# Recurrence matrices stored dense per state group, their products as 64 by 64 parts of the array, lag matrices spread by transfers

## What is computed

```python
def s5_mixer(u, lam_re, lam_im, log_dt, b_re, b_im, c_re, c_im, d, w_glu, b_glu):
    uf = u.astype(f32).reshape(bsz, L, S5_GROUPS, S5_GROUP)
    y = uf * d.astype(f32).reshape(S5_GROUPS, S5_GROUP)
    for direction in range(2):
        ...
        bu = jnp.einsum('blgh,gph->blgp', uf, b_bar)
        a = jnp.broadcast_to(lam_bar, bu.shape)
        _, state = lax.associative_scan(_linear_recurrence_op, (a, bu), axis=1,
                                        reverse=(direction == 1))
        ...
        y = y + jnp.real(jnp.einsum('blgp,ghp->blgh', state, c_mat))
    y = jax.nn.gelu(y.reshape(bsz, L, W_A))
```

## Time and profile before

| | |
|---|---|
| runs | 2553.88 us median, 2548.26 to 2555.88 (3 runs) |
| the profiled execution | 2550.92 us, its span 2549.4 us |
| mean granted TensorE clock | 0.991 |
| busy share: TensorE, its weight loads, VectorE, ScalarE, GpSimd | 98%, 81%, 72%, 50%, 6% |
| TensorE's share of the chain that ended last | 94% |
| HBM traffic | 161 GB/s over the span |

### The profile page before, as it was taken

One profiled execution on the slowest core, in us unless ns is written; L12 is line 12 of the kernel. 1 busy time (PEld: TensorE's weight loads), 2 busy tenths in 40 slices (PEclk: granted clock), 3 DMA queues, 4 the chain that ended last, 5 costly groups with the idle time before them and its releaser, 6 DMA issues.

```text
span 2549.4 us, 44643 instructions
## 1 busy us (share of the span) xinstructions
PE 2487.7 (98%) x15016; PEld 2053.9 (81%) x15016; DVE 1846.8 (72%) x3235; ACT 1273.7 (50%) x2364; POOL 142.6 (6%) x270
## 2 busy tenths in 40 slices
PE   6999999999999999999989999999999999999998
PEld 5888888887777778898778888888777777788986
DVE  7888888745777776556678888886367877765666
ACT  5556556634444444453465655555344434354535
POOL 2110000100000000000021000010000000000000
PEclk9999999999999999999999999999999999999998
DMA  7545445443454435555565544544444534365554
GB/s 253 175 157 165 160 160 164 152 147 136 156 168 134 138 110 187 189 173 175 166 206 162 164 160 159 167 156 145 149 151 150 175 112 149 115 193 189 171 177 145
DMA packets 117959, 411.86 MB, mean 162 GB/s; under 512 B 16484, under 2 KB 18586, under 8 KB 117584
## 3 DMA queue, kind: packets, MB, share of 16 engines
q1 hardware_dynamic: 107424, 391.17, 46.4%
q0 software_dynamic: 10416, 19.16, 2.3%
HBM read 403.97 MB, written 6.29 MB: 161 GB/s over the span
## 4 chain that ended last, share of the span: by engine, by line
PE 94%; DVE 3%; issue 2%; ACT 1%; PEldq 0%; DMA 0%; PEld 0%; DVEq 0%; ACTq 0%; POOL 0%; POOLq 0%
PE bank L1620 30%; PE bank L1660 21%; PE bank L1662 10%; PE bank L2008 7%; PE bank L1595 5%; PE bank L1577 4%; PE bank L1928 2%; PE bank L1793 2%; PE bank L1715 1%; PE bank L1698 1%; PE bank L1751 1%; PE bank L1942 1%; PE bank L1826 1%; PE bank L1908 1%; PE bank L1850 1%
## 5 line engine op out<-in xcount | busy, mean ns | idle before, releaser
L388 ACT ACTIVATE WH<-ring 128x512 fp32r<-128x512 f32 x1364 | 851.8, 631 | 1061.2 <-PE bank L1620 471.6
L402 DVE TENSOR_TENSOR WL<-ring,WH 128x512 fp32r<-128x512 f32 x852 | 573.3, 689 | 410.5 <-ACT WH L388 407.8
L1660 PE MATMUL bank<-XX,WH 128*128 128x512 f32 x2304 | 825.7, 402 | 29.4 <-DVE XX L573 15.2
L1662 PE MATMUL bank<-XX,WL 128*128 128x256 f32 x2304 | 646.3, 280 | 0.0
L1660 PEld LDWEIGHTS bank<-XX,WH 128*128 128x128 f32 x2304 | 436.0, 189 | 139.4 <-issue 18.8
L1620 PE MATMUL bank<-WH,XX 128*128 128x512 f32 x1536 | 487.4, 399 | 4.5 <-issue 3.4
L393 DVE TENSOR_TENSOR WL<-ring,WH 128x512 fp32r<-128x512 f32 x512 | 349.4, 688 | 122.5 <-ACT WH L388 117.2
L1662 PEld LDWEIGHTS bank<-XX,WL 128*128 128x128 f32 x2304 | 437.9, 190 | 0.0
L1620 PEld LDWEIGHTS bank<-WH,XX 128*128 128x128 f32 x1536 | 286.3, 189 | 82.3 <-issue 22.7
L1620 PE MATMUL bank<-WL,XX 128*128 128x512 f32 x768 | 300.6, 391 | 0.0
L1620 PEld LDWEIGHTS bank<-WL,XX 128*128 128x128 f32 x768 | 144.7, 188 | 31.4
(11 more groups left out here) (316 smaller groups left out, 3232.3 us busy)
## 6 DMA issues: line engine op xcount, KB each, us to landing
ring<-in_blocks SPq DMA_DIRECT2D x738, 512.0 KB, 3.3
ARENA<-in_bc POOLq DMA_DIRECT2D x2, 2048.0 KB, 8.3
ARENA<-in_decay POOLq DMA_DIRECT2D x8, 512.0 KB, 4.1
ARENA<-in_x SPq DMA_DIRECT2D x4, 512.0 KB, 8.2
u_scratch<-ARENA POOLq DMA_DIRECT2D x16, 128.0 KB, 3.0
ARENA<-u_scratch POOLq DMA_DIRECT2D x64, 32.0 KB, 2.9
y_scratch<-ARENA POOLq DMA_DIRECT2D x16, 128.0 KB, 2.7
ARENA<-y_scratch POOLq DMA_DIRECT2D x128, 16.0 KB, 2.0
```

The source lines that it names most:

```text
L388: nc.scalar.activation(wh[q], raw(which[0], q), ACT.Copy).then_inc(wh_ready[q], 1)
L402: vec.tensor_tensor(wl[q], raw(which[0], q), wh[q].bitcast(F32), ALU.subtract).then_inc(w_used[slot(which[0], half)], 1)
L1660: ins = mm(bank[b][:, :], h, xx[:, :, k, :], start=(k == 0), stop=(k == DT - 1), skip_group_check=True)
L1662: ins = mm(bank[b][:, 0:T], l, xh[:, k, :], start=False, stop=(k == DT - 1), skip_group_check=True)
```

## The change

It changes how the matrices of the recurrence stand in SBUF and in which parts of the array they are multiplied:

- E and F are stored dense: the two groups of a pair stand in the upper and lower 64 partitions, with the same columns. The zeros are gone; VectorE makes each part with one operation over 128 partitions where it took two over 64. Only the first step of E keeps a padded copy, EZ, for the lags (ScalarE, four small copies `first_step` per pass).
- The channels of a projection tile are permuted on the host (`by_class`) so that pairs 0, 2 stand in one half of the partitions and pairs 1, 3 in the other. `U4` is filled with 8 transfers per tile where there were 4, issued behind the write of the next tile.
- `turn()` makes 16 transposes of 64 rows, 64 wide, in one go; two evictions where there were four. `inputs()`, `direct()` and `outputs()` multiply 64 by 64 parts with 64 columns, dealt over the halves of rows and columns. Banks 2 and 3 now go by class and no more by real and imaginary part, so VectorE's rotation reads and writes with other strides.
- `lags()` is 64 wide. ScalarE evicts the 7 lags in one copy (LAG), GpSimd writes them to `lag_scratch` and reads them back with 8 transfers into M. The 16 window copies are gone.
- The direct part stands by itself between blocks 6 and 7, into banks 6 and 7. Waits of the interludes are put ahead of the last pair of the block before (`ahead`).

The order on TensorE becomes `block_at(0)`, `block_at(1)`, `turn()`, `block_at(2)`, `inputs()`, `block_at(3)`, `lags()`, `block_at(4)`, `block_at(5)`, `block_at(6)`, `direct()`, `block_at(7)`, `outputs()`.

```diff
-        E, ET, F, M = area(90, 8), area(98, 4), area(102, 10), area(112, 2)
+        E, EZ, ET, F, M = area(90, 4), area(94, 2), area(98, 4), area(102, 5), area(112, 1)
+        LAG = area(96, 1)[:, 0:LAGS * 16]
...
+                def load_input(m):
+
+                    pool.wait_ge(us_written[m % 2], layer * (8 * WT) + 16 * (m // 2 + 1))
+                    pool.sem_inc(us_landed, 1)
+                    by_step = u_scratch[layer, m].rearrange("(s n h) (t c) -> s t h n c", s=2, n=4, t=STEP)
+                    for s_ in range(2):
+                        for t in range(STEP):
+                            rows = slice(64 * s_ + 16 * t, 64 * s_ + 16 * t + 16)
+                            pool.dma_start(split(U4[rows, m * T:(m + 1) * T], 4), by_step[s_, t]).then_inc(u4_loaded, 16)
...
-                    pool.wait_ge(psum_free[7], read_out(layer, "s5", 7, ct))
+                    pool.wait_ge(psum_free[4], read_out(layer, "s5", 4, ct * 2 + 1))
+                    pool.dma_start(lag_scratch[ct], LAG).then_inc(lag_written, 16)
+                    pool.wait_ge(lag_written, layer * (16 * WT) + (ct * 16 + 16))
+                    by_half = lag_scratch[ct].rearrange("(s n h) x -> s h n x", s=2, n=4)
+                    for s_ in range(2):
+                        for t in range(STEP):
+                            rows = slice(64 * s_ + 16 * t, 64 * s_ + 16 * t + 16)
+                            pool.dma_start(split(M[rows, :], 4), by_half[s_][:, :, (STEP - 1 - t) * 16:(2 * STEP - 1 - t) * 16]).then_inc(m_ready, 16)
...
-                    for g in range(2):
-                        v.tensor_tensor(own(E, 0, g), flat(half(T1, 0), g), flat(half(T1, 1), g), ALU.subtract).then_inc(e_ready, 1)
+                    v.tensor_tensor(half(E, 0), half(T1, 0), half(T1, 1), ALU.subtract).then_inc(e_ready, 1)
...
-                    for q in range(PAIRS):
-                        for t in range(STEP):
-                            ins = window(q, t)
-                        if q < 2:
-                            make_wh(act, q, layer, B_S5 + 7, ct, 8)
-                    free(ins, 4)
+                    full(4, "s5", ct * 2 + 1)
+                    free(a.activation(LAG, bank[4][:, 0:LAGS * 16], ACT.Copy), 4)
...
+                        if k == DT - 1 and ahead is not None:
+                            ahead()
...
+                    def turn():
+
+                        for i in range(8):
+                            for g in range(2):
+                                ins = nc.tensor.transpose(bank[4 + g][:, i * 64:(i + 1) * 64], E[halves[g], i * P:(i + 1) * P], ident[halves[g], halves[g]])
...
+                    def inputs():
+
+                        for i in range(8):
+                            for s_ in range(2):
+                                for g in range(2):
+                                    o = bank[2 + s_][halves[g], i * HOPS:(i + 1) * HOPS]
+                                    ins = mm(o, ET[halves[s_], g * CW + i * 64:g * CW + (i + 1) * 64], uc(i % 2 * 2 + s_, g)[halves[s_], :], start=True, stop=True)
...
                     def lags():
...
+                                    f = part_of(F, r, d, q, 80)[:, d * 16:d * 16 + 64]
+                                    release(mm(bank[4][at_quarter(q), at:at + 64], part_of(EZ, r, d, q, 32), f, start=(d == r == 0), stop=False, skip_group_check=True))
...
+                    def lags_spread():
+
+                        pe.wait_ge(m_ready, layer * (128 * WT) + (ct * 128 + 128))
...
+                    def direct():
+
+                        for q in range(2):
+                            for g in range(2):
+                                for s_ in range(2):
+                                    at = slice((q * 2 + g) * 64, (q * 2 + g + 1) * 64)
+                                    ins = mm(bank[7 - g][halves[s_], q * HOPS:(q + 1) * HOPS], M[halves[s_], at], uc(q * 2, g)[halves[s_], :],
+                                             start=(q == 0), stop=False, skip_group_check=True)
...
                     def outputs():
...
+                        for q in range(2):
                             for d in range(2):
                                 for r in range(2):
+                                    for s_ in range(2):
+                                        for g in range(2):
+                                            f = part_of(F, r, d, 2 * q + s_, 80)[halves[g], (1 - d) * 16:(1 - d) * 16 + 64]
+                                            x_ = part_of(SP, r, d, 2 * q + s_, SEG)[halves[g], 2 * d:2 * d + HOPS]
+                                            ins = mm(bank[7 - g][halves[s_], q * HOPS:(q + 1) * HOPS], f, x_, start=False, stop=(d == 1 and r == 1), skip_group_check=True)
```

More of the change, by code:

```diff
@@ L1322, in _ @@
                     turned(1)
+                    act.wait_ge(zeroed, layer + 1)
+                    for g in range(2):
+                        for d in range(2):
+                            first_step(g, d).then_inc(ez_ready, 1)
                     make_wh(act, 0, layer, B_S5 + 3, ct, 8)
@@ L1355, in _ @@
                     act.wait_ge(y4_free, layer * WT + (ct + 1))
-                    full(7, "s5", ct)
-                    free(a.activation(Y4, bank[7][:, 0:T], ACT.Copy), 7)
+                    for g in range(2):
+                        full(7 - g, "s5", ct)
+                        into = Y4.rearrange("p (q g c) -> p q g c", q=2, g=2)[:, :, g, :]
+                        free(a.activation(into, split(bank[7 - g][:, 0:P], 2), ACT.Copy), 7 - g)
                     st.leave(WT)
@@ L1691, in turn @@
-                    def turn(q):
-                        b = 4 + q % 2
-                        if q == 0:
-                            pe.wait_ge(e_ready, layer * (4 * WT) + (ct * 4 + 4))
-                        take_bank(b, "s5", ct * (3, 2)[q % 2] + q // 2)
-                        for i in range(4):
-                            ins = nc.tensor.transpose(bank[b][:, i * P:(i + 1) * P], part_of(E, i % 2, i // 2, q, P), ident)
-                            if i < 3:
-                                release(ins)
-                        done(ins, b)
@@ L1703, in inputs @@
-                    def inputs(q):
-                        if q == 0:
-                            pe.wait_ge(uc_ready, layer * WT + (ct + 1))
-                            take_bank(2, "s5", ct)
-                            take_bank(3, "s5", ct)
-                        out_of(4 + q % 2, "s5", ct * (3, 2)[q % 2] + q // 2)
-                        for i in range(4):
-                            d, r = i // 2, i % 2
-                            for g in range(2):
-                                o = bank[2 + r][64 * g:64 * g + 64, (d * PAIRS + q) * HOPS:(d * PAIRS + q + 1) * HOPS]
-                                at = q % 2 * CW + i * P + 64 * g
-                                ins = mm(o, ET[:, at:at + 64], uc(q), start=True, stop=True)
-                                if q == PAIRS - 1 and d == g == 1:
-                                    done(ins, 2 + r)
+                        wide_block(j % 2, B_S5 + j, ct, 8, ahead=ahead)
@@ L2075, in weight_blocks @@
         [0, W, W, 3 * W, W, 512, 512, 64, W, 3 * D])
-    out = [block_of(column_tiles(w_in, seg(a_x, m))) for m in range(WT)]
+    by_class = np.arange(P).reshape(2, 2, 32).transpose(1, 0, 2).reshape(-1)
+    out = [block_of(column_tiles(w_in, a_x + m * P + by_class)) for m in range(WT)]
     out += [block_of(column_tiles(w_in, seg(b_u, m))) for m in range(24)]
```

216 lines of the change are left out of this document (114 added, 102 removed).

## The result

The changed kernel takes 2509.56 us (median of 3, 2506.62 to 2510.76) against 2553.88 (2548.26 to 2555.88): ratio 0.9828, interval 0.9806 to 0.9849, 44 us less. A second measurement of it, beside nine runs of the kernel before (median 2551.74), gave 2505.01 and a ratio of 0.9817 (0.9802 to 0.9832). Predicted were 2513, in 2498 to 2533.

A forecast was written before the change was run, and what follows sets the result against it. TensorE's own sequence bounds the kernel; interludes shrink from 7.86 to 5.31 us per pass, 2.55 gained, x 16 = 41 us, other terms zero: 2513 us against the median, range 2498 to 2533.

The forecast's parts named there:

- Rival D: Whole kernel: faster interludes only make TensorE wait for VectorE's low weights, nothing gained, 2554 us; chance 0.06.
- the zeros of the diff's striped operations, copies and scatter: VectorE's striped rotations, ScalarE's small copies and the 64-DMA input scatter stay hidden and cost TensorE zero.
- Row tiles overlap: Interludes: tiles one above the other in the array's rows work at once; turn 0.60, lags 0.70, direct 0.62 us.
- Rival A: Interludes: issue never beats the earlier sustained pace, 0.027 us a record; gain 23 us, 2531 us; chance 0.12.
- rival B: Interludes: row tiles don't work at the same time; gain 13 us, 2541 us; chance 0.07.
- the serial form: Direct products: upper and lower rows can't write one bank at once, 1.03 for 0.62 us, 6.6 us more, 2520.
- The issue price of 0.023 a record: Interludes: TensorE's sequencer needs 0.023 us per record, so inputs take 1.30 us and outputs 2.00.
- 0.4 us, counted as nothing: End of the stage: split Y4 puts some 0.2 us ahead of TensorE's squares, 0.4 us in the run, counted zero.
- The lag matrices' cover: Lag matrices' way through memory: 10.8 us, hidden behind 16.7 us of blocks, 5.9 us of slack.
- Rival C: Lag loads land one behind the other: chain 20.3 us against 16.7, slower than before at 2571 us; chance 0.03.
- Marks: Expected signs: pass 50.7 us, inputs 1.1 to 1.4, direct 0.6, branch about 1.1 us behind the first of outputs.
- the two signs of being wrong: The prediction is wrong if the blocks' rhythm, 0.35 us a pair, changes, or if another stage does.

The follow-up runs named there:

- The unrolled loop: Changed kernel with TensorE's loop over the eight passes written out, so no branch stands behind the outputs; 2497.06 us.
- the moved direct products: Changed kernel with the direct products, and their wait for the lag transfers, one block earlier, between blocks 5 and 6; 2570.28 us.
- the gap filled as well: Changed kernel with TensorE's loop written out and six idle products behind it, ahead of the wait for ScalarE's squares; 2496.52 us, ratio 0.9781.
- the inputs by rows: Changed kernel with all 16 input products on the upper 64 partitions dealt first, then all 16 on the lower; 2521.78 us.
- all by rows: Changed kernel with turn, inputs and outputs all dealt upper 64 partitions first, then lower; 2538.38 us.
- the one run where issue set the pace: Changed kernel with each of the 16 lag products cut into four of 16 columns; 2517.76 us.

## Why the prediction was right

**The bound.** TensorE's own sequence set the time, and the shortening of the interludes came through: 48.6 us shorter interludes, loops 46.7 shorter from first turn to last outputs, 44.3 of the run. VectorE, ScalarE and GpSimd cost nothing in the passes; TensorE's only idle time of a pass is the 0.48 at the loop's end. Rival D is out, and the zeros of the diff's striped operations, copies and scatter held.

**Row tiles overlap** (the step on which all rested, read from columns alone): right. Turn, lags and direct came within 0.04 of their terms. Rival A had 1.88 for the inputs and rival B 2.01; measured 1.09. The Trainium skill's floor of about 25 ns from start to start ("TensorE: Matmul & The Clock Gate", the part on the 56 ns gap) doesn't hold for such small tiles dealt over the array: 0.015 over 64 records in a row, 0.0093 over 136. Direct deals its products in turn to the upper and the lower rows, and both of such a pair write one bank; it took 0.612, two at a time, where the serial form would be 1.03. Gotcha 1 of the Trainium skill's "TensorEngine Tiling (Array Packing)", that row tiles can't access one bank at once, doesn't show in that row.

**The issue price of 0.023 a record: wrong.** It gave 1.30 for the inputs and 2.00 for the outputs; they took 1.09 and 1.63. I had read it from the sequencer's register work behind 16 records of the earlier trace rows and took the interval for the time of issuing. But that sequencer was held back by a full queue. In the trace of before, at 258.6, it has issued 16 of 32 records when two have started, and 0.42 us later, where its register work behind the last of them starts (L1544), all 32 when 14 have started. It is 14 ahead and then 18. These are the 14:

```profile
258.61:259.04 0.43, 0.42 (x14) 1.00 0.87 210
```

So the interval shows the array's pace of 0.029. The trace of before had this beside the row that I used. In the changed kernel the last output is issued 0.73 us behind the start of the first (the branch work, L1706, starts at 223.56), where 48 x 0.023 = 1.10 stood; from there to the block it is 0.91, as the 0.9 of the earlier trace rows has it, and 0.73 + 0.91 is the 1.64 of the outputs. The unrolled loop shows what is left without the branch: 1.09 for 64 records, where the array's 64 x 0.0145 + 0.15 is 1.08, with no issue in it. The end of the loop costs 0.54, where my 48 x 0.023 + 0.9 had it at 0.92 beyond the array. This term was too dear by 0.21 + 0.37 a pass, 9 us in the run.

**The end of the stage: a term that was missing.** "0.4 us, counted as nothing" stood there for the split copy. The idle time grew by 0.66 per layer, 1.3 us, and the clock fell behind it, 4.6 us. The 1.3 are the change's. The 4.6 can't be laid on it with certainty: the clock fell behind gaps of the old length too, in the runs above, and the kernel before may have been lucky in both layers. The idle time of before (2.37) stood in the trace; that such a gap can cost 1.5 to 3 us of half clock I didn't consider. The timelines of ScalarE and VectorE just ahead of the squares in the changed kernel show the chain that TensorE waits for.

```profile
477.12 1.91 ACT L1384 ACTIVATE ARENA<-ARENA 128x2048 f32<-128x2048 f32 x1 [0.48 <-DVE ARENA L725]
```
```profile
474.40 0.69 DVE L398 TENSOR_TENSOR WL<-ring,WH 128x512 fp32r<-128x512 f32 x1 [0.55 <-ACT WH L393]
476.00 0.69 DVE L398 TENSOR_TENSOR WL<-ring,WH 128x512 fp32r<-128x512 f32 x1 [0.91 <-ACT WH L393]
476.61 0.41 DVE L725 TENSOR_TENSOR ARENA<-ARENA,bank 128x256 f32 x1
```

The squares wait for ScalarE's long square (L1384), this for VectorE's add of block 7 (L725), and that stands behind the last quarter of the low weights (L398), which had waited 0.91 for ScalarE's high weights. Measured from the start of the last outputs, TensorE's outputs end 1.40 us earlier than before, and the squares can start only 0.74 earlier: ScalarE's and VectorE's queue does not end earlier by as much. At the last pass of a layer a part of TensorE's gain is idle time.

The two errors, 9 us too little and some 6 too much, partly cancel, and the forecast lies 3.4 us above the first measurement and 8 above the second. That it lies so near is in part luck.

**The lag matrices' cover: right in sign, wrong in size.** 16.7 us against 10.8 was the sum; the chain takes 11.7 to 14.3. The eviction and GpSimd's start took 1.0 for 0.8, the write 3.9 to 4.3 for 3.5, and the rest is the loads. The price came from the y transfers of one pass of before (10.0 us from write to last landing); over its 16 passes they took 9.6 to 12.3. TensorE never waited. One block earlier it would have lost all the gain, as the moved direct products show. Rival C (20.3 for the chain, 2571) names the right mechanism at a price that didn't come.

**Marks.** Pass 50.7: 50.52. Inputs near 1.1: the sequencer doesn't bind. The branch comes 0.73 behind the first of outputs, not 1.1. Direct 0.6. TensorE idle neither ahead of direct nor inside the blocks. Of the two signs of being wrong the rhythm of the blocks held (eight of them 45.72 for 45.60, about what the entry into turn takes), and the other came up: the squares, another stage, changed by 4.6 us. Not tried: what it is worth that TensorE's waits on matrices stand ahead of a block's last pair and not behind the block.

## What to carry to other kernels

Deal small products over all parts of the array in turn: the order of the loop was worth 23 to 27 of some 46 us here, and it costs nothing. An issue rate read from a sequencer whose queue is full is the array's rate; count how many records it stands ahead at both ends of the stretch, and take the rate only where the lead shrinks. When the bound engine gets faster, look at the places where it has to wait anyway: its lead turns into a longer idle time there, and the clock may fall behind such a gap.

## What the runs showed of the hardware

**Two paces of the same block.** A block is 16 pairs of the same records, and its pairs follow each other either in 346.7 or in 353.3 ns, from the block's start to the next interlude: 0.11 us a block. The timeline of the changed kernel above has three fast ones between lags and direct, 250.06 to 266.89 = 16.83. The same stretch with the loop unrolled:

```profile
246.44 0.50 PE L1683 MATMUL bank<-XX,WH 128*128 128x512 f32 x1
...
263.59 0.68 PE L1781 MATMUL bank<-ARENA 64*64 64x64 f32 x16
```

17.15. Of 124 blocks (all but the first two of each layer) 51 are slow before, 54 after (60 in its second profile), 96 with the loop unrolled, 97 with the gap filled as well, 99 with the inputs by rows, 100 with all by rows. It is not mere noise: behind the lags all 16 passes are fast in the first profile of the changed kernel and 15 in the second, and all 16 are slow with the loop unrolled. Blocks that follow each other without an interlude keep one pace. It decides over some 5 us. What selects the pace is open.

**The clock behind an idle time of 2.4 to 3.0 us** fell 16 times of 22 and stayed six times; the squares behind it took 4.96 to 6.61 us where it fell and 3.55 where it stayed.

**Loads on GpSimd's queue** can stop for 3.0 us between two issues, waiting for nothing shown, at the same two of sixteen passes in every run compared.

**TensorE's sequencer** stood 12 to 20 records ahead of the array at the ends of the inputs, lags and outputs, before and after the change, and 1 to 6 ahead in the one run where issue set the pace, at 0.0093 us a record.

**Entering the small tiling** from whole-array blocks took 0.21 where the step from record to record is 0.115: 0.1 us, which no row of before had alone.
